# Decode-sample attention groups placed between prompt tiles in both attentions of a two-layer streaming encoder

## The reference

```python
# layer 0, prompt and sample: scores of an indexer choose keys, the rest is masked
logits = einsum('bthd,btkhd->bhtk', q, k_chosen) * DH**-0.5 + t5_bias      # DH = 64
p = softmax(where(valid, logits, -inf))
out = einsum('bhtk,btkhd->bthd', p, v_chosen)
# prompt: 1024 queries over up to 1024 own keys
# sample: 32 queries over 2048 past keys (cache_a_k, cache_a_v) and 32 new ones
# layer 1, prompt: each chunk of 64 sees itself and the 8 chunks before
logits = einsum('bthd,bshd->bhts', q, k) * DH**-0.5 + rel_bias
# layer 1, sample: 32 queries over 512 past keys (cache_c_k, cache_c_v) and 32 new ones
```

## Time and profile before

| what | value |
|---|---|
| median of 3 runs | 3065.2 us |
| span of the profiled execution | 3063.2 us |
| time around the span (median minus span) | 2.0 us |
| TensorE busy | 2910.1 us (95%) |
| VectorE busy | 1613.1 us (53%) |
| GpSimd busy | 1292.9 us (42%) |
| ScalarE busy | 958.8 us (31%) |

### The profile page before, as it was taken

How to read it: one execution, slowest core, us unless ns; L and a number is a source line. 1 busy time by engine, 2 the same in 40 slices (tenths; PEclk the granted TensorE clock), 3 DMA queues, 4 the chain that set the end, 5 groups by cost and what they waited for, 6 DMA issues and landing times. The chain is left out here.

```text
span 3063.2 us, 60271 instructions
## 1 busy us (share of the span) xinstructions
PE 2910.1 (95%) x25097; PEld 2707.8 (88%) x25097; DVE 1613.1 (53%) x2967; ACT 958.8 (31%) x2005; POOL 1292.9 (42%) x1053
## 2 busy tenths in 40 slices
PE   6999999996789999999999999999899999999998
PEld 5859999765689999999999999866689999999998
DVE  6399999655646644434346400056537644444445
ACT  3341111355433433332101311266525333332001
POOL 2111223382533877776334232100124877775334
PEclk9999999998899999999999999999999999999999
DMA  5816763533241122224221232253121222214222
GB/s 214 252 67 215 239 206 134 166 127 112 100 171 51 58 83 77 84 84 138 87 84 63 80 103 100 74 196 103 50 86 49 70 77 84 84 68 156 79 75 73
DMA packets 160464, 338.82 MB, mean 111 GB/s; under 512 B 21032, under 2 KB 94528, under 8 KB 152192
## 3 DMA queue, kind: packets, MB, share of 16 engines
q1 hardware_dynamic: 120720, 281.74, 27.3%
q10 hardware_dynamic: 39472, 53.21, 4.9%
HBM read 268.30 MB, written 79.49 MB: 114 GB/s over the span
## 5 line engine op out<-in xcount | busy, mean ns | idle before, releaser
L109 PE MATMUL tr_acc<-tr_quad_hi,ah_ring_hi 128*128 128x264 f32 x2432 | 694.5, 286 | 8.3 <-DVE tr_kept L1188 2.2
L111 PE MATMUL tr_acc<-tr_quad_hi,ah_ring_lo 128*128 128x264 f32 x2432 | 692.6, 285 | 0.0
L110 PE MATMUL tr_acc<-tr_quad_lo,ah_ring_hi 128*128 128x264 f32 x2432 | 690.2, 284 | 0.0
L575 POOL TENSOR_TENSOR ah_ring_lo<-ah_raw,ah_ring_hi 128x512 fp32r<-128x512 f32 (+1 forms) x402 | 555.0, 1386 | 159.5 <-ACT ah_ring_hi L918 146.5
L109 PEld LDWEIGHTS tr_acc<-tr_quad_hi,ah_ring_hi 128*128 128x128 f32 x2432 | 458.5, 189 | 10.6 <-DVE tr_kept L1188 2.6
L110 PEld LDWEIGHTS tr_acc<-tr_quad_lo,ah_ring_hi 128*128 128x128 f32 x2432 | 458.7, 189 | 0.1
L111 PEld LDWEIGHTS tr_acc<-tr_quad_hi,ah_ring_lo 128*128 128x128 f32 x2432 | 458.2, 188 | 0.0
L573 POOL CAST ah_ring_hi<-ah_raw 128x512 fp32r<-128x512 f32 (+1 forms) x162 | 102.2, 631 | 591.3 <-PE tr_acc L111 525.3
L109 PE MATMUL tr_acc<-tr_part_hi,ah_ring_hi 128*128 128x352 f32 x1038 | 335.5, 323 | 2.0 <-DVE tr_kept L1226 2.0
L110 PE MATMUL tr_acc<-tr_part_lo,ah_ring_hi 128*128 128x352 f32 x1038 | 332.8, 321 | 0.0
L111 PE MATMUL tr_acc<-tr_part_hi,ah_ring_lo 128*128 128x352 f32 x1038 | 332.5, 320 | 0.0
(11 more groups left out here) (397 smaller groups left out, 6421.3 us busy)
## 6 DMA issues: line engine op xcount, KB each, us to landing
f_ada_w<-in_w_ada_dram SPq DMA_DIRECT2D x48, 1024.0 KB, 5.5
scratch_inner<-tr_kept ACTq DMA_DIRECT2D x88, 264.0 KB, 2.3
tr_staged<-scratch_inner SPq DMA_DIRECT2D x44, 528.0 KB, 4.2
ah_raw<-in_w_gate_dram SPq DMA_DIRECT2D x44, 512.0 KB, 3.6
ah_raw<-in_w_up_dram SPq DMA_DIRECT2D x44, 512.0 KB, 4.5
ah_raw<-in_w_down_dram SPq DMA_DIRECT2D x64, 256.0 KB, 3.3
f_raw<-in_w_dram SPq DMA_DIRECT2D x24, 512.0 KB, 8.0
out_z_dram<-f_stage ACTq DMA_DIRECT2D x60, 176.0 KB, 1.9
```

The lines of the kernel that those rows point to most:

```text
L109: pe.matmul(out, w_hi, hi, start=start, stop=False)
L110: pe.matmul(out, w_hi, lo, start=False, stop=False)
L111: return pe.matmul(out, w_lo, hi, start=False, stop=stop)
L575: pool.tensor_tensor(lo[:, 0:width], own, hi[:, 0:width].bitcast(F32), ALU.subtract).then_inc(w_ready, 1)
```

## The change

The list of steps now holds two kinds of items, prompt tiles and sample groups. A sample group enters the pipeline behind the tiles given in `after`: 15 and 27 in layer 0, 15, 31, 47 and 55 in layer 1. Its dots, logits, exponentials, turns and values take the same places relative to its own step as a tile's, and the loop has last_of + 5 steps. The second loop is gone. Further edits:

- In layer 0 the dots with the 32 new keys (the tail piece) go into a turn bank; in both layers the value sums of a group go into a turn bank instead of `out`, and VectorE's scaling frees it.
- Layer 0 has one set of past keys and values for the sample. The second group's are loaded into it after the prompt output of pair 1 is stored and the first group's dots and value sums are done.
- The sample's masks are added behind tile `after[0] // 2` = 7 instead of 16.
- ScalarE issues both stores of a group's output; SyncE issues none of them.
- The head of the recurrence is spread: VectorE's bounds and gains behind tiles 16, 20 and 22, the sigmoids on ScalarE in the two steps after the last tile, `queries` on VectorE in the last but one step.

```diff
+        self.tail = past >= 1024
+        self.pieces = [(lo, lo + 1024) for lo in range(0, past, 1024)] if self.tail else [(0, self.keys)]
+        self.after, self.masks_after = after, after[0] // 2
...
+    for u in range(U):
+        steps.append(("tile", u))
+        if u in side.after:
+            steps.append(("side", side.after.index(u)))
...
             def side_loads(g):
-                sp.dma_start(s_k[g][:], side.k_past[2 * g:2 * g + 2].rearrange("c p n -> p c n")).then_inc(s_k_in[g], 16)
+                own = g % own_sides
+                if g >= own_sides:
+                    sp.wait_ge(dots_done, dots_after[step_of["side", g - own_sides]])
+                sp.dma_start(s_k[own][:], side.k_past[2 * g:2 * g + 2].rearrange("c p n -> p c n")).then_inc(s_k_in[g], 16)
...
-                if u == U // 2:
+                if u == side.masks_after:
                     side_masks()
...
+        def dots_free(pe, s):
+            if s and (wide(s) or wide(s - 1)):
+                pe.wait_ge(logits, sums_before[s])
+            elif s >= 2:
+                pe.wait_ge(logits, sums_before[s - 1])
...
-            for s in range(G + 2):
-                if s < G:
-                    side_scores(s)
-                if 1 <= s <= G:
-                    for j in range(len(quads)):
-                        side_turns(s - 1, j)
-                    side_values(s - 1)
-                if s >= 2:
-                    side_turn_out(s - 2)
...
+            for s in range(last_of + 5):          # VectorE
+                own = [j for j in range(turns_of(s - 2)) if not by_act[turn_no[s - 2, j]]]
+                if tile(s) is not None:
+                    logit(s, 0)
+                elif group(s) is not None:
+                    side_logit(s, 0)
+                    if side.tail:
+                        side_tail(group(s))
...
+                if group(s - 3) is not None:
+                    side_scale(group(s - 3))
+                if tile(s) is not None and not widening:
+                    logit(s, 1)
+                elif group(s) is not None:
+                    for p in range(1, len(side.pieces)):
+                        side_logit(s, p)
+                    side_top(s)
...
+            for s in range(last_of + 5):          # ScalarE
+                if tile(s) is not None:
+                    exp(s, 1)
+                elif group(s) is not None:
+                    side_exp(group(s))
                 for j in own:
                     if j >= 2:
                         copy(s - 2, j)
+                if group(s - 4) is not None:
+                    side_out(group(s - 4))
+                if head and s == last_of:
+                    head.decay_sigmoid(act)
```

More of the change, by code:

```diff
@@ L2107, with __init__ @@
 class SampleSide:
[L2111 removed]
+    def __init__(self, k_past, v_past, past, skew, length, shift, mask_dram, after):
         self.k_past, self.v_past, self.past = k_past, v_past, past
@@ L2154, in attention_phase @@
     U = len(units)
+    G = heads // 4
     blocks = [keys[i] // P for _, i in units]
[L2156 to L2165, removed]
@@ new lines, in attention_phase, with item, tile, group @@
+    last_of = len(steps)
+    step_of = {at: s for s, at in enumerate(steps)}
+    def item(s):
+        return steps[s] if 0 <= s < last_of else (None, None)
+    def tile(s):
+        return item(s)[1] if item(s)[0] == "tile" else None
+    def group(s):
+        return item(s)[1] if item(s)[0] == "side" else None
+    def turns_of(s):
+        if tile(s) is not None:
+            return (2 * blocks[tile(s)] + 3) // 4
+        return len(quads) if group(s) is not None else 0
+    def sums_of(s):
+        return 2 if tile(s) is not None else len(side.pieces)
@@ L2460, in side_values @@
                             right = s_v_new[:, 256 * g + DH * j:256 * g + DH * j + DH]
-                        last = pe.matmul(out[g % 2][S * j:S * j + S, 0:DH], left, right, start=c == 0, stop=c == side.blocks)
-                last.then_inc(s_out, 1)
+                        last = pe.matmul(turn[n % 2][S * j:S * j + S, 0:DH], left, right, start=c == 0, stop=c == side.blocks)
+                last.then_inc(turned, 1)
             def side_turn_out(g):
                 n = side_out_no[g]
-                pe.wait_ge(s_scaled, g + 1)
@@ L2493, in _, with logit @@
+                if tile(s - 3) is not None:
+                    values(s - 3)
+                elif group(s - 3) is not None:
+                    side_values(s - 3)
+                if ends_quad(s - 3):
+                    spread_inverse(tile(s - 3) // 4)
+                for j in range(2, turns_of(s - 2)):
+                    turns(s - 2, j)
+                if group(s - 4) is not None:
+                    side_turn_out(group(s - 4))
         @block.vector
         def _(dve):
-            def logit(u, hd):
+            def logit(s, hd):
+                u = tile(s)
@@ new lines, in side_tail, with side_top @@
+            def side_tail(g):
+                n = tail_no[g]
+                dve.wait_ge(turned, n + 1)
+                dve.tensor_tensor_reduce(side_prob(g)[:, side.keys - S:side.keys], turn[n % 2][:, 0:S], s_bias[g][:, side.keys - S:side.keys],
+                                         -DH ** -0.5, 3.0e38, ALU.add, ALU.min, s_least[:, g, 2:3]).then_inc(dve_copied, 1)
+            def side_top(s):
+                g = group(s)
+                parts = len(side.pieces) + side.tail
+                dve.wait_ge(logits, sums_before[s + 1])
+                if side.tail:
+                    dve.wait_ge(dve_copied, tail_no[g] + 1 - act_no[tail_no[g] + 1])
+                dve.tensor_reduce(s_least[:, g, 3:4], s_least[:, g, 0:parts], AX_X, ALU.min).then_inc(s_top, 1)
```

382 lines of the change are left out of this document (191 added, 191 removed).

## The result

The changed kernel takes 3072.6 us (median of 7 runs, 3069.6 to 3075.9), the kernel before 3065.2 in the same session (7 runs, 3063.5 to 3067.9). The ratio is 1.0025, 95% interval 1.0015 to 1.0035: slower by 7.4 us. I had forecast 3066.7, 1.5 us slower, and "no measurable change". The time lies in the range I gave (3058 to 3075). But the interval doesn't reach down to 1, and the difference lies past the 6.1 us within which I had counted a result as none, on the slower side, which I had given 0.19.

What follows compares the result with a forecast made beforehand. TensorE, busy 95% of the span, was taken as the bound. Span 3063.2 + 2.0 to the median + 4.4 for layer 0 - 2.9 for layer 1 = 3066.7 us, no measurable change; range 3058 to 3075 for 8 in 10.

Steps and rivals of the forecast that it cites:

- layer 0: tail removed: Layer 0, from the last prompt output to the recurrence's first GpSimd operation: 29.7 us go.
- behind the last tile (store, barrier): Layer 0's end: the last output store, no longer hidden, and the barrier cost 4.0 us together, bounds 3.6 to 6.2.
- group 1 with its waits: Layer 0 behind tile 15: 9.7 us of TensorE's work plus waits of 2.4 and 0.8 for ScalarE, 12.9 us.
- group 2 with its waits: Layer 0 behind tile 27: 9.7 us of TensorE's work plus waits of 1.35 and 0.65, 11.7 us.
- masks: Layer 0, tile 8: GpSimd's two mask additions delay its extra and so TensorE, 4.7 us, bounds 0 and 9.2.
- costs of nothing: Layer 0: head's bounds and gains, reload and value sums in a turn bank cost nothing; each under 1 us if uncovered.
- drain: Layer 0's end: ScalarE issues the second group's two stores and computes a sigmoid before the last copies, 0.8 us, bounds 0 and 3.
- layer 1: Layer 1: 22.8 us removed, 9.1 us of store, load and barrier and 10.8 us of four groups added, -2.9 us.
- rival C: Start of trunk and recurrence: colder after TensorE's idleness, 0 to 3 us; chance 0.62 together with the forecast.
- ScalarE's copy waits behind the exponential: Layer 0, first group: the third copy of tile 14 stands behind the group's exponential, so TensorE waits 2.4 us.
- A: Rival for the whole sum: the items cost TensorE only their own work, 10.7 us less, 3056.0 us; chance 0.17.
- B: Rival at layer 1's groups and layer 0's second: ScalarE late at each, 2.4 us apiece, 3076.7 us; chance 0.17.

Runs made afterwards that it cites:

- e1: Changed kernel with GpSimd's mask additions behind tile 15 instead of tile 7: 3066.0 us, ratio 1.0000 to the kernel before.
- e8: Changed kernel with ScalarE's third copy of tile 14 ahead of the first group's exponential: 3069.5 us, ratio 1.0011 to the kernel before.
- e2: Changed kernel with the recurrence's bounds behind tile 24's logits instead of tile 20's: 3069.6 us, ratio 1.0011 to the kernel before.
- e3: Changed kernel with each of the bounds' two 128x4 products done as four 128x1 operations: 3070.0 us, ratio 1.0015 to the kernel before.
- e9_all: Changed kernel with masks behind tile 15, bounds behind tile 24, ScalarE's third copy ahead of the first group's exponential: 3059.5 us, ratio 0.9977 to the kernel before.
- e6: Changed kernel with the sample's bias loaded ahead of the second pair's tensors, masks still behind tile 7: 3079.7 us, ratio 1.0039 to the kernel before.
- c0_after: The changed kernel run again with no edit, as the mark for the other runs: 3074.5 us, ratio 1.0029 to the kernel before.

## Why the time was in the range and the sum was not right

The measured items are distances between the same instructions in the two first profiles, beside the prediction's terms; the trunk is the mean of all profiles. The items of layer 0 add up to 10.5 us, the lengths of the two attentions differ by 10.7.

| step | forecast | measured |
|---|---|---|
| layer 0: tail removed | -29.7 | -29.7 |
| behind the last tile (store, barrier) | 4.0 | 3.8 |
| group 1 with its waits | 12.9 | 11.3 |
| group 2 with its waits | 11.7 | 10.3 |
| masks | 4.7 | 8.6 |
| head's bounds ("costs of nothing") | 0, under 1 | 5.3 |
| drain | 0.8 | 0.9 |
| layer 0 | +4.4 | +10.5 |
| layer 1 | -2.9 | -1.3 |
| trunk behind layer 1 (rival C) | 0 to 3, outside the sum | +1.7 in the mean, +0.5 in the first profile |

*What was right.* The structure of the sum: groups cost TensorE nearly their full work in the loop, the store is exposed, the masks delay tile 8's extra, ScalarE's copy waits behind the exponential (2.1 us for 2.4). e1 and e8 each took one of these away, and attention 0 followed. The direction was right as well: 1.5 us slower was forecast, 7.4 came.

*Groups priced too dear.* The two groups were 3.0 us cheaper than forecast. I had taken the values at 3.27 us from the earlier trace rows and called it "at full clock". It was not: the granted clock in that row is 0.58, and the second group's 125 value matmuls in the same tail take 1.98 us at 1.00 (stretch, PE, PEld, DVE, ACT, POOL, clock, DMA, GB/s, the kernel before):

```profile
730.25:733.50 3.25, 3.25 (x132) 3.16 (x135) 0.00 (x0) 0.00 (x0) 0.00 (x0) 0.58 0.02 5
737.29:739.30 2.01, 1.98 (x125) 1.82 (x126) 1.01 (x10) 2.00 (x2) 0.00 (x0) 1.00 0.04 8
```

In the loop they take 1.99 us. That is 1.3 us for each group, most of the 3.0.

*The step that failed* is "Costs of nothing": the head's bounds and gains fall into VectorE's waits, under 1 us if the cover went. It cost 5.3 us in the first profile, 4 to 5 by e2 and e3. I took the durations of 0.15 and 0.16 us from a place where GpSimd had been idle for 39 us (0.00 for POOL in the first of the earlier trace rows, and the 48.47 us ahead of 746.19 in the earlier trace rows) and moved them beside its unbroken additions without asking what they share. The kind of operation decides: the products with two SBUF inputs waited, the 128x1 operations that replaced them in e3 did not.

*The step that was mis-sized* is the masks: 8.6 instead of 4.7, inside my bound of 9.2. GpSimd's wait for the bias was 2.3 us where I had 0.4; and behind a wait of 6.2 us come about 2 us for the lower clock, which none of my terms had. Without these two (5.3 and 3.9) layer 0 would have come to +1.3, under my +4.4 by the 3.0 us of the cheaper groups, and the whole kernel to no measurable change.

*Luck.* That the time stayed in the range is in part luck. Layer 0 cost 9.2 us that I had not counted; 3.0 came back through the groups, for a reason that I had wrong, and in the first profile the stretch from the recurrence to the second attention was 2.0 us shorter by accident. Layer 1 gave 1.6 us less than forecast, 1.2 of it in its groups (3.0 us each for 2.7).

*Small sums.* The 3.7 us of work behind the first group add up to 3.9, so the wait would be 2.2 (2.1 measured); 1.3 less 0.78 is 0.5, not 0.65; 614.1 less 609.9 is 4.2, not 4.3; and three transfers at 2 us instead of 2.6, 2.7 and 5.1 would be 4.4 us less, not about one. The forecast hangs on none of them.

*Rivals.* A, the groups without waits, fell, though e9_all shows that moving three things nearly gives its time (3059.5, forecast 3056.0). B, ScalarE late at every group, fell: in layer 1 a group costs 3.0 us, and at the second group TensorE waits for VectorE. C was put down as worth 0 to 3 us. At the trunk's start behind layer 1 it is 0.8 us in the mean, from 0.2 to 1.0; the rest of the trunk's 1.7 us arises at its end and is not what C described. Behind layer 0 no profile shows it above the scatter there.

*Left open.* How much of the masks' 8.6 us is the bias that lands late: e6 did not separate it, and in c0_after GpSimd waited 1.4 us for it instead of 2.3 and the 8.6 us stayed, as the time at the lower clock was longer. When the clock falls after a wait of about 3.3 us: e8 and c0_after differ in it with the same wait. And why the clock at the trunk's end goes with layer 1's code.

## What to carry to other kernels

A small operation moved under cover keeps its duration only if the cover doesn't hold what it needs: look at the operand kinds of the moved instruction and at what the other engines run there (here additions of 2 us on GpSimd), not only at whether its own engine is idle. When work is folded into a loop, ask of every helper engine's work that moves with it whose next result it delays; here three one-line moves (masks, bounds, a copy) turned 8.4 us slower into 6.9 us faster. A row taken as the price of some work needs the granted clock beside it: 3.27 us at 0.58 were not the 1.99 of full clock. And a stretch gained at a phase's end counts only together with the next phase: the 1.8 us gained in front of the trunk stand against a trunk that was 1.7 us longer, half of it at its start.

## What the runs showed of the chip

- A 128x4 VectorE product of two SBUF tensors took 0.15 us with GpSimd idle and 1.79 to 2.29 us beside GpSimd's additions, ending within 0.1 us of the end of one. A 128x4 operation with constants waited too (0.68 us for 0.17, e3), and two of 128x16 with a constant (0.42 and 0.50 us for 0.17, e2). Reciprocals, 128x1 operations with a scalar, and logits that read PSUM did not.
- A wait of 3.35 us ahead of the same dots was followed by 3.36 us of dots at a granted clock of 0.50 in c0_after and by 1.77 us at 1.00 in e8_act_order, whose earlier wait of 2.1 us had been taken out. A wait of 2.6 us at the kernel's end was followed by the lower clock in some profiles (last twelve matmuls 2.9 us) and by full clock in others (1.7 us).
- The 128 value matmuls of a group took 3.27 us at a granted clock of 0.58 and 1.99 us at full clock. Which PSUM bank they write made no difference: into `out`, 125 of them took 1.98 us at 1.00.
